# The first expert layer: the results of every other pair of experts go as rows to a scratch in DRAM and are fetched by token at the end

## The chip, the cores and the metric

The kernel runs on one core of one Trainium2 chip. The metric is the device time of one execution in microseconds (us). Shown is the median of three runs.

## The reference

Two transformer blocks are computed, each two layers deep, on 256 tokens of width 1024 with 256 tokens of context beside them, all in float32. What matters here is the mixture of experts that follows the mixer in both layers of the second block:

```
g_idx = argmax(x @ wg + bg)                  # one of 4 groups
top_p, top_e = top_k(softmax(e_logits), 2)   # two of its 8 experts
weights = g_w * top_p / sum(top_p)
hb = silu(xb @ w1[e]) * (xb @ w3[e])         # w1, w3: 1024 x 512
y = hb @ w2[e]                               # w2: 512 x 1024
out = zeros.at[tok].add(y * weights)
```

So every token goes to two of 32 experts, both of one group of eight. In the first expert layer there are 512 tokens (256 tokens and 256 of the context), in the second 256. The weights of one expert are 6 MB, those of one layer 192 MB, and each is read once.

## The kernel before

The program is a chain of blocks, one for each step of the network; a block ends when all engines have reached its end. The code touched is the function `experts`, which runs for the first expert layer (512 tokens, `by_rows` true) and for the second (256 tokens).

The router gives for each token and expert a rank (`RK`): the place that the token takes in the expert's list, or a number far too large where it doesn't go there. An expert has 64 slots (`CAP`) in a round; with these inputs one round does. Two experts make a pair (128 slots, one per partition), two pairs make a turn (`b` is 0 and 1 in it), and eight turns make the layer. The text calls the four experts of a turn e0 to e3; e0 and e1 are the pair b = 0.

For one pair:

- `pick` (VectorE) compares slot numbers with ranks into `SEL`; `indices` (TensorE) multiplies that by the tokens' numbers; `index` (VectorE) turns the product into 128 integers; `fetch` (the GpSimd queue) gathers 128 rows of 4 KB by them from the scratch `token_rows` in DRAM. `gather` (TensorE) turns those rows into `XGT`.
- For each of the two experts: `hidden` multiplies by w1 and w3 (two halves of the array side by side), ScalarE takes the silu, VectorE multiplies (`multiply`, L2399), `turn_hidden` transposes, ScalarE copies (`h_turned`), `outputs` multiplies by w2, and `y_out` copies the result, a row for each slot, to `Y2`.
- The results go back to their tokens by a product: VectorE makes the picks again, multiplied by the tokens' weights (`SELW`, L2452), TensorE transposes them (L2262), ScalarE copies them to `SWT` (L2339), and `scatter` (L2233) multiplies `Y2` by `SWT` in eight products of 128 x 512, four after the first expert's `hidden` and four after the second's. They are those of the pair before, so they lie beside the silu of the present one. `add` (L2407) adds each product, times a gate, to `X`.

After the loop one more `scatter` and `add` treat the last pair. Between them stand the squares of `X` (L2343) and their sum over all features (`sum_squares`, L2267) for the next normalisation.

The weights come in tiles of 1 MB, six per expert (`parts`): four for `hidden`, two for `outputs`. There are 16 homes for tiles; the first eight are used twice in a turn. SyncE issues all 24 loads of a turn in the order of use, each when its home's tile of before has been used:

```
for e, part in parts:
    n, lap = spot(e, part)
    sp.wait_ge(*freed(n, turns * r + i, lap))
    sp.dma_start(homes[n], weights[4 * i + e, part]).then_inc(loaded[numbers[n]].sem, 16)
```

In the trace the fetches of rows are on queue q0, the loads on q1, and the stores that ScalarE issues on q10.

Of the kernel before, what the change touches and what calls it, by code (L numbers as in the profile page):

```python
# [16 lines left out]
P = 128  # L17
# [35 lines left out]
          ("prior", EPG), ("rounds", 8), ("stream", 2), ("eps", 1), ("token", NT), ("cos_rows", 2 * ROPE), ("sin_rows", 2 * ROPE),  # L53
# [16 lines left out]
def constants():  # L70
# [52 lines left out]
    put("rounds", np.tile(np.arange(8) * CAP, (P, 1)))  # L123
    put("stream", p[:, None] % 32 == np.arange(2)[None, :])
# [35 lines left out]
def build(nc, io, out):  # L160
# [22 lines left out]
    token_rows = nc.dram_tensor("token_rows", (T, D), F32).ap()  # L183
    rows_in = [Signal(nc, f"rows_in{b}", 0) for b in range(2)]
# [20 lines left out]
    for name in ("inputs_in", "stored", "dve_step", "act_step", "squared", "summed", "rooted", "normed",  # L205
# [14 lines left out]
                 "y_copied", "weighed"):  # L220
# [1775 lines left out]
    def experts(join, layer, moe, t, by_rows):  # L1996
# [12 lines left out]
        XG = BIG[:, 0:2 * D].rearrange("p (b n) -> p b n", b=2)  # L2009
        ahead = 3 if by_rows else 2  # L2010
# [64 lines left out]
        with nc.Block() as block:  # L2075
# [5 lines left out]
            @block.gpsimd  # L2081
            def _(pool):
                join.multiplied(pool)
                nc.gpsimd.memset(Y2[:, 1, :], 0.0).then_inc(sig("cleared").sem, 1)
                nc.gpsimd.memset(SWT, 0.0).then_inc(sig("cleared").sem, 1)
                if by_rows:
                    def fetch(g, b):

                        pool.wait_ge(sig("indexed").sem, sig("indexed").at(g))
                        pool.sem_inc(sig("index_seen").sem, 1)  # L2090
                        nc.gpsimd.indirect_dma_start(XG[:, b, :], None, token_rows,
                                                     bass.IndirectOffsetOnAxis(INDEX[b][:], 0)).then_inc(rows_in[b].sem, 16)

                    pool.wait_ge(sig("rows_kept").sem, sig("rows_kept").at(16 * nt))
                    fetch(1, 1)
                    every = rounds(pool)
                    with pool.Fori(0, every) as r, pool.Fori(0, turns) as i:
                        for b in range(2):
                            fetch(2 * (turns * r + i) + b + 2, b)

            @block.sync
            def _(sp):
# [15 lines left out]
                if by_rows:  # L2118
                    sp.wait_ge(sig("rows_kept").sem, sig("rows_kept").at(16 * nt))
                    sp.wait_ge(sig("gathered").sem, sig("gathered").at(2))  # L2120
# [16 lines left out]
            def _(pe):  # L2137
# [26 lines left out]
                def gather(g, c, b, use):  # L2164

                    if by_rows and use is not None:
                        pe.wait_ge(rows_in[b].sem, rows_in[b].at(16 * (use + 1)))
                        for k in range(4 * c, 4 * c + 4):
                            last = pe_.transpose(PB[:, 4 + c, (k % 4) * P:(k % 4 + 1) * P], XG[:, b, k * P:(k + 1) * P], IDENT)
                    else:  # L2170
                        pe.wait_ge(sig("picked").sem, sig("picked").at(g + 1))
                        for k in range(4 * c, 4 * c + 4):
                            for a in range(nt):
                                last = pe_.matmul(PB[:, 4 + c, (k % 4) * P:(k % 4 + 1) * P], ATK[:, a, k * P:(k + 1) * P],  # L2174
                                                  SEL[:, a, :], start=a == 0, stop=a == nt - 1)
                    last.then_inc(sig("gathered").sem, 1)

                def indices(g):

                    pe.wait_ge(sig("picked").sem, sig("picked").at(g + 1))  # L2180
                    pe.wait_ge(sig("indexed").sem, sig("indexed").at(g - 1))
                    pe.wait_ge(sig("pick_copied").sem, sig("pick_copied").at(g - 2))
                    for a in range(nt):
                        last = pe_.matmul(PB[:, 3, T - 2:T - 1], SEL[:, a, :], con("token")[:, a:a + 1],
                                          start=a == 0, stop=a == nt - 1)
                    last.then_inc(sig("indices_made").sem, 1)
# [51 lines left out]
                gather(0, 0, 0, None)  # L2238
                gather(0, 1, 0, None)
                if by_rows:  # L2240
                    indices(1)
                every = rounds(pe)
                with pe.Fori(0, every) as r, pe.Fori(0, turns) as i:
                    turn = turns * r + i
                    for b in range(2):
                        g = 2 * turn + b
                        hidden(turn, 2 * g, g, 2 * b, b)
                        if by_rows:
                            indices(g + 2)
                        scatter(g, 1 - b, 0)  # L2250
                        turn_hidden(2 * g, 0)
                        gather(g + 1, 0, 1 - b, turn)
# [4 lines left out]
                        gather(g + 1, 1, 1 - b, turn)  # L2257
                        if by_rows:
                            pe.wait_ge(sig("indexed").sem, sig("indexed").at(g + 2))
# [19 lines left out]
            def _(act):  # L2279
# [4 lines left out]
                def keep_rows(a):  # L2284
                    act.wait_ge(sig("token_copied").sem, sig("token_copied").at(a + 1))
                    act.dma_start(token_rows[a * P:(a + 1) * P, :], ATK[:, a, :]).then_inc(sig("rows_kept").sem, 16)

                for a in range(nt):
# [3 lines left out]
                    if by_rows and a:  # L2292
                        keep_rows(a - 1)
                if by_rows:
                    keep_rows(nt - 1)
# [51 lines left out]
            def _(dve):  # L2347
# [41 lines left out]
                def index(g, b, use):  # L2389

                    dve.wait_ge(sig("indices_made").sem, sig("indices_made").at(g))
                    dve.wait_ge(rows_in[b].sem, rows_in[b].at(16 * use))
                    dve.wait_ge(sig("gathered").sem, sig("gathered").at(2 * g - 2))
                    dve_.tensor_scalar(INDEX[b][:], PB[:, 3, T - 2:T - 1], 0.25, None, ALU.add) \
                        .then_inc(sig("indexed").sem, 1)

# [36 lines left out]
                if by_rows:  # L2433
                    index(1, 1, 0)
                    pick(2)
# [3 lines left out]
                with dve.Fori(0, every) as r:  # L2439
                    with dve.Fori(0, turns) as i:  # L2440
                        for b in range(2):
# [3 lines left out]
                            if by_rows:  # L2445
                                index(g + 2, b, turns * r + i + b)
# [11 lines left out]
                            if not by_rows:  # L2458
                                dve.wait_ge(sig("gathered").sem, sig("gathered").at(2 * g + 4))
# [9 lines left out]
               group_exped=1, second_in=1, second_exped=1, dve_step=router_steps, rounds_in=1, cleared=2, logits_kept=1, logits_flipped=1,  # L2469
               rows_kept=16 * nt if by_rows else 0, squared=KD, summed=1)  # L2470
        if moe:
            return

        counted = used + loaded + [sig(n) for n in ("picked", "gathered", "indices_made", "indexed", "index_seen", "xg_copied",
                                                    "expert_silu", "expert_h", "h_flipped", "h_copied", "y_copied",
                                                    "weighed", "pick_flipped", "pick_copied", "scattered", "added",
                                                    "rank_in")]
        with nc.Block() as block:
            @block.sync
# [157 lines left out]
```

## Time and profile before

| | |
|---|---|
| median of 3 runs | 2930.11 us (2929.3 to 2930.96) |
| span of the profiled execution, first to last instruction | 2926.7 us |
| TensorE busy | 2765.9 us |
| VectorE, ScalarE, GpSimd busy | 1170.7, 707.9, 19.1 us |
| moved by DMA | 663.34 MB, mean 227 GB/s |

The page has no time of its own for the profiled execution apart from its span; the span lies 3.4 us under the median, and that is what lies around it. The page cuts the span into 40 slices of 73 us. The first expert layer is slices 23 to 30 (1603 to 2176 us), the second slices 34 to 40. In the rows, PE is TensorE, PEld its loading of weights, DVE VectorE, ACT ScalarE, POOL GpSimd and SP SyncE. A matmul in float32 stands as two instructions in the trace.

### The profile page before, as it was taken

The page shows a single profiled execution, that of the slowest core. Times are in us where ns is not written, and L with a number is a line of the kernel's source. Part 1 is how long each engine was busy: PE and PEld are TensorE (multiplying, and loading weights), DVE is VectorE, ACT ScalarE, POOL GpSimd, SP SyncE. Part 2 cuts the span into 40 slices and gives each one's busy share as a digit, 9 for nine tenths or more (in the row PEclk, how much of TensorE's full clock was granted, in tenths as well). Part 3 has the DMA queues.
Part 4 walks back from the last instruction along what each step waited for, and adds up shares of the span by engine and source line. Part 5 has one row for each costly group of instructions (what it writes and reads, how often), then busy time and mean ns, then how long its engine had stood idle before and what let it go on. Part 6 is the DMA issues. An engine that isn't in the chain of part 4 may idle for free. (4 is left out here: it accounts for less than half of the span.)

```text
span 2926.7 us, 33922 instructions
## 1 busy us (share of the span) xinstructions
PE 2765.9 (95%) x12378; PEld 1541.7 (53%) x12378; DVE 1170.7 (40%) x2630; ACT 707.9 (24%) x1347; POOL 19.1 (1%) x25
## 2 busy tenths in 40 slices
PE   5999999999999998999978999999989988999998
PEld 3555344444467777888543433333337774444444
DVE  2342477770146666771342333333343323222222
ACT  2343200000055553000251221212132222222222
POOL 0000000000000000000000000000000000000000
PEclk9999999999999999999999999999999999999999
DMA  6133455552322213775005699999923337999995
GB/s 254 74 115 115 172 216 238 234 215 82 119 73 73 67 50 136 308 291 209 0 15 225 239 401 402 406 401 402 403 113 136 138 115 284 421 422 422 421 422 235
DMA packets 101826, 663.34 MB, mean 227 GB/s; under 512 B 10608, under 2 KB 19056, under 8 KB 25072
## 3 DMA queue, kind: packets, MB, share of 16 engines
q1 hardware_dynamic: 98720, 651.22, 56.3%
q0 software_dynamic: 2448, 8.91, 0.8%
q10 hardware_dynamic: 576, 2.10, 0.2%
q8 instruction: 54, 0.88, 0.1%
q14 instruction: 28, 0.23, 0.0%
HBM read 659.04 MB, written 3.15 MB: 226 GB/s over the span
## 5 line engine op out<-in xcount | busy, mean ns | idle before, releaser
L622 PE MATMUL PB<-A,RING 128*128 128x512 f32 (+1 forms) x1408 | 459.0, 489 | 9.7 <-ACT A L499 9.7
L622 PEld LDWEIGHTS PB<-A,RING 128*128 128x128 f32 x1408 | 269.6, 192 | 199.2 <-issue 175.0
L397 DVE SCALAR_TENSOR_TENSOR WORK<-RING,MORE 128x1024 f32<-128x1024 f32 x288 | 335.4, 1220 | 20.3 <-ACT MORE L636 10.9
L451 PE MATMUL PB<-BIG,RING 128*128 (+2 forms) x928 | 310.7, 497 | 5.7 <-PEq L590 3.3
L2399 DVE TENSOR_TENSOR BIG<-BIG,PB 64x512 f32<-64x512 f32 x64 | 44.1, 690 | 671.7 <-ACT BIG L2309 671.7
L451 PEld LDWEIGHTS PB<-BIG,RING 128*128 128x128 f32 x928 | 175.9, 190 | 139.4 <-issue 128.8
L2199 PE MATMUL PB<-RING,BIG 128*64 128x512 f32 x1024 | 225.4, 592 | 0.6 <-issue 0.6
L2233 PE MATMUL PB<-BIG 128*128 128x512 f32 (+1 forms) x544 | 202.1, 504 | 11.8 <-DVE X L2407 6.9
L2407 DVE SCALAR_TENSOR_TENSOR X<-PB,MODS,X 128x256 f32<-128x256 f32 x408 | 173.3, 478 | 35.6 <-PE PB L2233 34.1
L2233 PEld LDWEIGHTS PB<-BIG 128*128 128x128 f32 x544 | 93.6, 189 | 120.6 <-issue 60.1
L514 DVE SCALAR_TENSOR_TENSOR X<-PB,MODS,X 128x256 f32<-128x256 f32 x72 | 32.4, 479 | 297.7 <-PE PB L479 296.9
L2199 PEld LDWEIGHTS PB<-RING,BIG 128*64 128x64 f32 x1024 | 75.0, 137 | 144.4 <-issue 144.3
L641 ACT ACTIVATE RS<-PB 128x512 f32<-128x512 f32 (+1 forms) x44 | 21.6, 491 | 422.1 <-PE PB L622 422.1
L2320 ACT ACTIVATE BIG<-PB 64x512 f32<-64x512 f32 x128 | 75.8, 592 | 193.7 <-PE PB L2220 192.9
L2309 ACT ACTIVATE BIG<-PB 64x512 f32<-64x512 f32 x64 | 37.7, 589 | 347.1 <-PE PB L2199 347.1
L1625 PE MATMUL PB<-A,RING 128*128 128x512 f32 x256 | 115.2, 605 | 6.2 <-ACT A L499 6.2
L2220 PE MATMUL PB<-SPARE,BIG 128*64 128x512 f32 x512 | 116.9, 598 | 1.8
L2199 PE MATMUL PB<-CST,BIG 128*64 128x512 f32 x256 | 115.3, 592 | 0.0
L2199 PE MATMUL PB<-RS,BIG 128*64 128x512 f32 x256 | 115.1, 592 | 0.0
L492 ACT ACTIVATE WORK<-X 128x512 f32<-128x512 f32 (+1 forms) x48 | 26.8, 559 | 345.2 <-DVE X L514 345.2
L1625 PEld LDWEIGHTS PB<-A,RING 128*128 128x128 f32 x256 | 48.7, 195 | 63.4 <-issue 61.8
L2174 PE MATMUL PB<-WORK,BIG 128*128 128x128 f32 x608 | 77.0, 283 | 2.3 <-DVE WORK L2385 2.3
(355 smaller groups left out, 3480.7 us busy)
## 6 DMA issues: line engine op xcount, KB each, us to landing
RING<-moe_w SPq DMA_DIRECT2D x160, 1024.0 KB, 10.7
RING<-ada_rows SPq DMA_DIRECT2D x72, 1024.0 KB, 6.8
RING<-ffn_w SPq DMA_DIRECT2D x66, 1024.0 KB, 4.8
SPARE<-moe_w SPq DMA_DIRECT2D x64, 1024.0 KB, 8.1
CST<-moe_w SPq DMA_DIRECT2D x32, 1024.0 KB, 7.7
RS<-moe_w SPq DMA_DIRECT2D x32, 1024.0 KB, 9.7
MORE<-moe_w SPq DMA_DIRECT2D x32, 1024.0 KB, 12.9
A<-moe_w SPq DMA_DIRECT2D x32, 1024.0 KB, 16.8
```

Of the source, the lines that this page charges most:

```text
L397: dve_.scalar_tensor_tensor(out=JUNK[:, n % 4, :], in0=RING[:, s, b * D:(b + 1) * D], scalar=1.0, in1=WIDE[:, side // 2, w, :], op0=ALU.mu ...
L451: last = pe_.matmul(PB[:, m, 0:tp], tile(s, 2, D)[:, r, m * P:(m + 1) * P], src(2 * i + r), start=first and r == 0, stop=False)
L622: last = pe_.matmul(PB[:, 2 * s + j, 0:t], tile(s, KD, P, j * KD * P)[:, k, :], A[:, k, 0:t], start=k == 0, stop=k == KD - 1)
L1625: last = pe_.matmul(PB[:, 1 + d, :], w[:, k, :], A[:, k, :], start=k == 0, stop=k == KD - 1)
L2174: last = pe_.matmul(PB[:, 4 + c, (k % 4) * P:(k % 4 + 1) * P], ATK[:, a, k * P:(k + 1) * P], SEL[:, a, :], start=a == 0, stop=a == nt - 1)
L2199: last = pe_.matmul(PB[m * CAP:(m + 1) * CAP, 0, :], XGT[:, b, k, slots_of(e % 2)], spot_tile(n_, 4, T)[:, k % 4, :], start=k == 0, stop=k ...
L2220: last = pe_.matmul(PB[m * CAP:(m + 1) * CAP, 2, :], HB[:, e % 2, k, :], spot_tile(n_, 2, D)[:, k % 2, m * T:(m + 1) * T], start=k == 0, s ...
L2233: pe_.matmul(result(m), Y2[:, b, m * P:(m + 1) * P], SWT[:, 0:t], start=True, stop=True) \
L2309: act_.activation(HS[CAP:P, e % 2, :], PB[0:CAP, 0, :], ACT.Silu).then_inc(sig("expert_silu").sem, 1)
L2320: last = act_.activation(Y2[slots_of(e % 2), b, m * T:(m + 1) * T], PB[m * CAP:(m + 1) * CAP, 2, :], ACT.Copy)
L2399: dve_.tensor_tensor(HS[0:CAP, j, :], HS[CAP:P, j, :], PB[CAP:P, 0, :], ALU.mult) \
L2407: last = dve_.scalar_tensor_tensor(out=X[:, m, half(w)], in0=result(m)[:, half(w)], scalar=piece(2 + moe, 5, m, w), in1=X[:, m, half(w)], ...
```

## The change

In the first expert layer only, which now has a function of its own (`experts_by_rows`; `experts` keeps the second layer):

- The pair b = 1 of each turn goes back as before, by `scatter` and `add`, now in the next turn's pair b = 0 and after the loop. `SELW`, its transposes and `SWT` are made once a turn.
- The pair b = 0 doesn't go by a product. ScalarE issues a store of its 128 rows (512 KB) from `Y2[:, 0]` to a scratch in DRAM, `result_rows` (`store_rows`).
- Before the loop VectorE computes for each token and each of its two experts the row in the scratch and the weight, zero where the expert is of a pair b = 1 (`places_back`).
- After the last fetch of the loop GpSimd's queue waits for the last store and for the last use of four homes (`MORE` and `RING` 0 and 1), and issues eight gathers of 128 rows (512 KB each) into them (`BACK`). VectorE weighs and sums the two rows of each token (`mix_rows`), and TensorE adds them to the last pair's products in PSUM, transposed by a product with the identity.
- After the loop all eight products are made in banks of their own; the sums of squares stand behind all of them.
- Two constants of 32 columns are added, and six semaphores to those cleared after the layer.

The second expert layer's code does what it did.

```diff
@@ gpsimd
+                with pool.Fori(0, every) as r:
+                    with pool.Fori(0, turns) as i:
                         for b in range(2):
                             fetch(2 * (turns * r + i) + b + 2, b)
+                    pool.wait_ge(sig("placed").sem, sig("placed").at(r + 1))
+                    for n in (10, 11, 0, 1):
+                        pool.wait_ge(used[n].sem, used[n].at(turns * r + turns))
+                    pool.wait_ge(sig("rows_stored").sem, sig("rows_stored").at(16 * (turns * r + turns)))
+                    pool.sem_inc(sig("index_seen").sem, 1)
+                    for a in range(nt):
+                        for c in range(2):
+                            nc.gpsimd.indirect_dma_start(
+                                BACK[c][:, a, :], None, result_rows,
+                                bass.IndirectOffsetOnAxis(RETURN[c * nt + a][:], 0)).then_inc(rows_back[a].sem, 16)
...
@@ tensor
+                            hidden(turn, 2 * g, g, 2 * b, b)
+                            indices(g + 2, turn)
+                            if b == 0:
+                                scatter(r, i, turn, 0)
+                            turn_hidden(2 * g, 0)
+                            gather(g + 1, 0, 1 - b, turn)
+                            outputs(turn, 2 * g, 2 * b)
+                            hidden(turn, 2 * g + 1, g, 2 * b + 1, b)
+                            if b == 0:
+                                scatter(r, i, turn, 1)
+                            turn_hidden(2 * g + 1, 1)
+                            gather(g + 1, 1, 1 - b, turn)
+                            if b == 1:
+                                pe.wait_ge(sig("indexed").sem, sig("indexed").at(g + 2))
+                                pe.wait_ge(sig("weighed").sem, sig("weighed").at(turn + 1))
+                                for a in range(nt):
+                                    last = pe_.transpose(PB[:, 3, a * P:(a + 1) * P], SELW[:, a, :], IDENT)
+                                last.then_inc(sig("pick_flipped").sem, 1)
+                            outputs(turn, 2 * g + 1, 2 * b + 1)
+
+                    done = each_round * r + KD * turns
+                    pe.wait_ge(sig("y_copied").sem, sig("y_copied").at(2 * pairs * (r + 1)))
...
+                    for m in range(KD):
...
+                        pe_.matmul(tail_result(m), Y2[:, 1, m * P:(m + 1) * P], SWT, start=True, stop=False)
+                        for a in range(nt):
+                            if m == 0:
+                                pe.wait_ge(sig("rows_mixed").sem, sig("rows_mixed").at(nt * r + a + 1))
+                            last = pe_.matmul(tail_result(m)[:, a * P:(a + 1) * P], BACK[0][:, a, m * P:(m + 1) * P], IDENT,
+                                              start=False, stop=a == nt - 1)
+                        last.then_inc(sig("scattered").sem, 1)
@@ scalar
+                def store_rows(i, g):
+                    act.wait_ge(sig("y_copied").sem, sig("y_copied").at(2 * g + 2))
+                    act.dma_start(result_rows.rearrange("(e s) n -> e s n", s=CAP)[bass.ds(2 * i, 2)],
+                                  Y2[:, 0, :]).then_inc(sig("rows_stored").sem, 16)
@@ vector
+                def places_back(c, r):
+
+                    flat = WIDE.rearrange("p a g e -> p a (g e)")
+                    every_token = [P, nt, NE]
+                    c(dve_.tensor_tensor(HOME, RK[:, :, 0:NE], con("row_base").unsqueeze(1).broadcast_to(every_token), ALU.add))
+                    for n, (one, share) in enumerate(((O1, M1), (O2, M2))):
+                        c(dve_.tensor_tensor(WIDE, wide(one, full, 2), wide(G1, full, 3), ALU.mult))
+                        c(dve_.tensor_tensor(flat, flat, con("in_rows").unsqueeze(1).broadcast_to(every_token), ALU.mult))
+                        for op, limit in ((ALU.is_ge, 0.0), (ALU.is_lt, float(CAP))):
+                            c(dve_.scalar_tensor_tensor(out=flat, in0=RK[:, :, 0:NE], scalar=limit, in1=flat, op0=op, op1=ALU.mult))
+                        c(dve_.tensor_reduce(SHARES[:, n], flat, AX.X, ALU.add))
+                        dve_.tensor_tensor(SHARES[:, n], SHARES[:, n], share[:, :, 0], ALU.mult)
+                        c(dve_.tensor_tensor(flat, flat, HOME, ALU.mult))
+                        c(dve_.tensor_reduce(PLACE[:, n], flat, AX.X, ALU.add))
+                        for a in range(nt):
+                            last = dve_.tensor_scalar(RETURN[n * nt + a][:], PLACE[:, n, a:a + 1], 0.25, None, ALU.add)
+                    last.then_inc(sig("placed").sem, 1)
+
+                def mix_rows(c, r, a):
+                    dve.wait_ge(rows_back[a].sem, rows_back[a].at(32 * (r + 1)))
+                    c(dve_.tensor_scalar(BACK[0][:, a, :], BACK[0][:, a, :], SHARES[:, 0, a:a + 1], None, ALU.mult))
+                    dve_.scalar_tensor_tensor(out=BACK[0][:, a, :], in0=BACK[1][:, a, :], scalar=SHARES[:, 1, a:a + 1],
+                                              in1=BACK[0][:, a, :], op0=ALU.mult, op1=ALU.add) \
+                        .then_inc(sig("rows_mixed").sem, 1)
```

How the order of instructions moves, at three places. In these rows `CST` is the tile with the identity, `BIG` the one that holds `XGT`, `Y2`, `SWT` and the hidden values, and `x4` counts equal instructions in a row; a matmul stands as one row here.

TensorE in the pair b = 1, from the indices to the outputs of e2, before:

```order
L2184 MATMUL PB<-CST,WORK 128x1 x4
L2232 ISA
L2233 MATMUL PB<-BIG 128x512
L2232 REGISTER_ALU
L2233 MATMUL PB<-BIG 128x512
L2232 REGISTER_ALU
L2233 MATMUL PB<-BIG 128x512
L2232 REGISTER_ALU
L2233 MATMUL PB<-BIG 128x512
L2207 MATMUL PB<-CST,BIG 128x128 x4
L2169 MATMUL PB<-CST,BIG 128x128 x4
L2218 REGISTER_ALU
```

and in the change:

```order
L2212 MATMUL PB<-CST,WORK 128x1 x4
L2235 MATMUL PB<-CST,BIG 128x128 x4
L2197 MATMUL PB<-CST,BIG 128x128 x4
L2246 REGISTER_ALU
L2248 MATMUL PB<-SPARE,BIG 64x512 x8
```

The four products of `scatter` between the indices and the transposes of the hidden values are gone; after e3's `hidden` four more are gone in the same way.

TensorE after the loop, before:

```order
L2233 MATMUL PB<-BIG 128x512
L2267 MATMUL PB<-WORK,CST 128x512 x2
L2232 REGISTER_ALU
L2233 MATMUL PB<-BIG 128x512
L2232 REGISTER_ALU
L2233 MATMUL PB<-BIG 128x512
L2232 REGISTER_ALU
L2233 MATMUL PB<-BIG 128x512
L2232 REGISTER_ALU
L2233 MATMUL PB<-BIG 128x512
L2267 MATMUL PB<-WORK,CST 128x512 x6
```

and in the change, its last two products of eight:

```order
L2301 MATMUL PB<-BIG 128x512
L2305 MATMUL PB<-CST,MORE 128x128 x4
L2300 REGISTER_ALU
L2301 MATMUL PB<-BIG 128x512
L2305 MATMUL PB<-CST,MORE 128x128 x4
L2269 REGISTER_ALU
L2269 COMPARE_AND_BRANCH
L2311 MATMUL PB<-WORK,CST 128x512 x8
```

Each product of 128 x 512 has four of 128 x 128 behind it, and all eight sums of squares stand at the end where six stood.

The GpSimd queue after the loop, in the change (before, the loop was its last work in this layer):

```order
L2104 DMA BIG<-token_rows,INDEX 128x1024
L2111 REGISTER_ALU
L2111 COMPARE_AND_BRANCH
L2114 REGISTER_ALU
L2116 ISA
L2116 REGISTER_ALU x2
L2117 ISA
L2121 DMA MORE<-result_rows,RETURN 128x1024
L2121 DMA RING<-result_rows,RETURN 128x1024
L2121 DMA MORE<-result_rows,RETURN 128x1024
L2121 DMA RING<-result_rows,RETURN 128x1024
```

Of the eight gathers four are shown; they stand behind the last fetch of the loop.

## Rows read from the trace of the kernel before

**Rows 1.** The page: DMA busy in tenths, and GB/s, in 40 slices.
```profile
DMA  6133455552322213775005699999923337999995
GB/s 254 74 115 115 172 216 238 234 215 82 119 73 73 67 50 136 308 291 209 0 15 225 239 401 402 406 401 402 403 113 136 138 115 284 421 422 422 421 422 235
```

**Rows 2.** Windows of one turn each, first expert layer: turns 3 and 8.
```profile
core 0: us, PE busy (x) PEld busy (x) DVE busy (x) ACT busy (x) POOL busy (x), PEclk, DMA share, GB/s
1769.40:1834.40 65.00, 63.69 (x282) 25.14 (x280) 21.69 (x58) 13.28 (x23) 1.87 (x2) 1.00 1.00 404
2094.40:2159.40 65.00, 63.69 (x282) 25.00 (x278) 21.94 (x59) 13.28 (x23) 1.87 (x2) 1.00 0.61 244
```

**Rows 3.** Waits of SyncE's queue, 1700 to 2130 us: total, times, longest.
```profile
SPq L2131 <- PE PB L2199: 230.5, 39, 12.7
SPq L2131 <- PE PB L2220: 103.2, 26, 6.8
```

**Rows 4.** Waits of TensorE (without its weight loads), 1770 to 2100 us.
```profile
PE PB L2233 <- DVE X L2407: 4.3, 10, 0.4
```

**Rows 5.** A window of the second expert layer's loop; columns as above.
```profile
2500.00:2800.00 300.00, 300.00 (x1570) 146.40 (x1567) 61.96 (x163) 64.83 (x116) 0.00 (x0) 1.00 1.01 421
```

**Rows 6.** DMA queues, 1770 to 2100 us: packets, MB, share of 16 engines.
```profile
q1 hardware_dynamic: 17573, 127.96, 96.1%
q0 software_dynamic: 1440, 5.24, 3.9%
```

**Rows 7.** DMA queues, 1620 to 1636 us: the four stores of `token_rows`.
```profile
q10 hardware_dynamic: 576, 2.10, 34.1%
```

**Rows 8.** Timeline of TensorE, pair b = 1: start, us, what.
```profile
1874.82 4.06 PE L2233 MATMUL PB<-BIG 128*128 128x512 f32 x8
1878.72 0.60 PE L2207 MATMUL PB<-CST,BIG 128*128 128x128 f32 x4
...
1890.32 1.99 PE L2233 MATMUL PB<-BIG 128*128 128x512 f32 x4
...
1894.56 0.60 PE L2207 MATMUL PB<-CST,BIG 128*128 128x128 f32 x4
```

**Rows 9.** Timeline of VectorE, the same stretch.
```profile
1874.67 0.69 DVE L2399 TENSOR_TENSOR BIG<-BIG,PB 64x512 f32<-64x512 f32 x1 [10.87 <-ACT BIG L2309]
1891.08 0.69 DVE L2399 TENSOR_TENSOR BIG<-BIG,PB 64x512 f32<-64x512 f32 x1 [9.51 <-ACT BIG L2309]
```

**Rows 10.** Timeline of VectorE, routing and start of the loop.
```profile
1630.22 0.29 DVE L2430 TENSOR_TENSOR WORK<-WORK 128x128 f32<-128x128 f32 x1
1647.14 0.69 DVE L2399 TENSOR_TENSOR BIG<-BIG,PB 64x512 f32<-64x512 f32 x1 [7.63 <-ACT BIG L2309]
```

**Rows 11.** Windows: the first turn's middle, and the end of the last loads.
```profile
1669.00:1677.00 8.00, 8.00 (x40) 2.67 (x38) 0.00 (x0) 1.40 (x3) 0.00 (x0) 1.00 0.09 10
2133.00:2134.00 1.00, 1.00 (x7) 0.19 (x3) 0.00 (x0) 0.00 (x0) 0.00 (x0) 1.00 0.16 66
```

**Rows 12.** Timeline of GpSimd, the last fetch.
```profile
2136.34 0.94 POOL L2091 DMA_INDIRECT BIG<-token_rows,INDEX  x1 [31.56 <-DVE INDEX L2394]
```

**Rows 13.** Timeline of TensorE, the end of the layer.
```profile
2155.96 3.65 PE L2220 MATMUL PB<-A,BIG 128*64 128x512 f32 x16
2161.08 4.07 PE L2233 MATMUL PB<-BIG 128*128 128x512 f32 x8 [1.47 <-ACT BIG L2320]
2170.52 5.31 PE L2267 MATMUL PB<-WORK,CST 128*128 128x512 f32 x12
```

**Rows 14.** Groups: line, engine, operation, shapes, count, busy us, mean ns.
```profile
L397 DVE SCALAR_TENSOR_TENSOR WORK<-RING,MORE 128x1024 f32<-128x1024 f32 x288 | 335.4, 1220 | 20.3 <-ACT MORE L636 10.9 <-DVE WORK L397 5.9 <-issue 0.9
L1499 DVE TENSOR_SCALAR WORK<-WORK,SMALL 128x512 f32<-128x512 f32 x32 | 14.1, 483 | 0.6
```

**Rows 15.** Timeline of TensorE: products of 128 x 128, second expert layer.
```profile
2609.00 1.95 PE L2174 MATMUL PB<-WORK,BIG 128*128 128x128 f32 x16
```

**Rows 16.** Windows after the layer's end: a pause of TensorE and its clock.
```profile
2180.00:2185.00 5.00, 0.00 (x0) 0.00 (x0) 4.41 (x6) 0.69 (x1) 0.00 (x0) 0.54 0.79 281
```

More of the change, by code:

```diff
@@ new lines, in experts_by_rows, with wide, across, spot @@
+        assert free[0] <= SLOT
+        router_steps, row_steps = 35, 19
+        weights = io["moe_w"][moe]
+        WTF = WT.rearrange("p a g e -> p a (g e)")
+        pairs = NE // 2
+        turns = pairs // 2
+        def wide(x, shape, axis):
+            return x.unsqueeze(axis).broadcast_to([P] + shape)
+        def across(x, n):
+            return x.broadcast_to([P, nt, n])
+        def spot(e, part):
+            n = PARTS * e + part
+            return (n, 0) if n < 12 else (n - 12, 1) if n < 20 else (n - 8, 0)
@@ new lines, in spot_tile, with freed, laps, result @@
+        def spot_tile(n, k, w):
+            return homes[n].rearrange("p (k n) -> p k n", k=k)
+        def freed(n, turn, lap):
+            return used[numbers[n]].sem, used[numbers[n]].at(turn * laps(n) + lap)
+        def laps(n):
+            return 2 if n < 4 * PARTS - SPOTS else 1
+        fit = T // t
+        def result(m):
+            return PB[:, 6 + m // fit % 2, m % fit * t:(m % fit + 1) * t]
+        each_round = KD * (turns + 1)
+        def tail_result(m):
+            return PB[:, 1 + m % 7, :]
@@ new lines, in experts_by_rows, with _, experts, take @@
+        with nc.Block() as block:
+            @block.sync
+            def _(sp):
+                for s in counted:
+                    sp.sem_clear(s.sem)
+                    sp.sem_inc(s.sem, FIRST)
+        for s in counted:
+            s.base = FIRST
+    def experts(join, layer, moe, t):
+        nt, streams = t // P, t // S
+        ATK = BIG[:, 0:NT * D].rearrange("p (a n) -> p a n", a=NT)
+        o = NT * D
+        def take(n):
+            nonlocal o
+            o += n
+            assert o <= FB * T
+            return BIG[:, o - n:o]
+        ahead = 2
@@ L2162, in _, with gather @@
                 last.then_inc(sig("ranked").sem, 1)
[L2164 to L2175, printed above, removed]
[L2176 to L2186 removed]
+                def gather(g, c):
+                    pe.wait_ge(sig("picked").sem, sig("picked").at(g + 1))
+                    for k in range(4 * c, 4 * c + 4):
+                        for a in range(nt):
+                            last = pe_.matmul(PB[:, 4 + c, (k % 4) * P:(k % 4 + 1) * P], ATK[:, a, k * P:(k + 1) * P],
+                                              SEL[:, a, :], start=a == 0, stop=a == nt - 1)
+                    last.then_inc(sig("gathered").sem, 1)
                 def hidden(turn, n, g, e, b):
```

461 lines of the change are left out of this document (394 added, 67 removed).

## The prediction

> **What bounds the kernel now.** I read the slices first, then the layer turn by turn, then who waits for whom. The slices [rows 1] show both expert layers with the DMA engines at nine tenths or more: 401 to 406 GB/s in the first, 420 to 422 in the second. So the first thing to settle is whether the first layer's loop waits for TensorE or for the weights.
>
> A window of one turn [rows 2] shows TensorE busy 63.69 of 65.0 us and the DMA share at 1.00. Both look full. The waits tell them apart: TensorE waits for no DMA at all, only for VectorE's adds, 4.3 us in 330 [rows 4], while SyncE, which issues the loads, waits for TensorE to free a home for 333.7 of 430 us [rows 3]. So today TensorE sets the turn of 65.0 us. But the transfers have almost nothing to spare. The second layer shows what 24 loads cost when nothing else is moved: 421 GB/s at a share of 1.01 [rows 5], so 1.049 MB take 2.49 us and 24 of them 59.8 us. The first layer's turn leaves 5.2 us for its two fetches of rows, 2.6 us each, and reports the engines full. The fetches' own packets explain only a part: 3.9% of 330 us for ten of them [rows 6] is 1.29 us each. The rest, 1.3 us a fetch, is either what a fetch costs the loads beside it or small gaps while TensorE holds homes back; the rows don't separate them. This is the number on which the sum hangs.
>
> **What the change takes from TensorE in the loop.** In the pair b = 1 the four products after e2's `hidden` run from 1874.82 and the transposes behind them start at 1878.72 [rows 8]. Without the products these would wait for VectorE's multiplication, which ends at 1874.67 + 0.69 = 1875.36 [rows 9]: 3.4 us less, not 3.9. After e3 the transposes move from 1894.56 [rows 8] to 1891.77 [rows 9]: 2.8 us less. The four transposes of `SELW` that go in b = 0 are at most 0.4 us. TensorE alone would need 65.0 - 6.6 = 58.4 us a turn. Eight turns save 53 us, and the loop, whose last outputs end at 2159.6 [rows 13], would end at 2107.
>
> **What the transfers allow.** They don't allow that. The engines stand still from 1669 to 1677 us (share 0.09, [rows 11]), since all homes are full until e2's `hidden` of turn 1 frees some; nothing before that point gets faster, so this gap stays. From 1677 on 7 x 24 = 168 tiles are loaded, with 14 fetches, until 2133.3 ([rows 11]: share 0.16 of the slice that begins at 2133): 168 x 2.49 = 418.3, and 38.0 over, 2.7 us a fetch. The change adds a store of 512 KB a turn, seven of which fall in this stretch (the first one falls in the gap or before). A store's own packets are 34.1% of 16 us for four [rows 7], 1.36 us each. The weights would be in at 1677 + 418.3 + 14f + 7s. With f and s at their own packets (1.29, 1.36) that is 2122.9; with 2.7 for each it is 2152.0. Even the lower one is after 2107, so in the change the loop follows the DMA engines: this is where the gain of TensorE goes. I take f = 1.9 and s = 1.6, about the middle for the fetch, because the loads' backlog will be deep and the gaps should vanish, and nearer its packets for the store, because no descriptors are made by GpSimd for it. That gives 1677 + 418.3 + 26.6 + 11.2 = 2133.1, against 2133.3 now.
>
> **The gathers at the end.** They stand behind the last fetch, which GpSimd issues at 2136.34 now, 23 us ahead of the last outputs [rows 12, 13]. In the change that is some 17 us ahead of the last weight, so fetch and gathers compete with the last loads and all share one set of engines: together they end nine transfers later, wherever they interleave. With 1.9 us each that is 2133.1 + 17.1 = 2150.2, and about 1 us to the semaphore: 2151.2. GpSimd issues one in 0.94 us [rows 12], eight in 8 us, so the queue isn't the limit.
>
> **After the loop.** For the last 128 tokens VectorE needs two passes over 1024 columns, 2 x 0.48 and 1.22 us [rows 14]: 2153.4. TensorE has then done the first product and the other three parts. The seven that are left cost each 4.07 / 4 = 1.0 us for the wide one [rows 13] and half of 1.95 us, 1.0, for its four narrow ones [rows 15]; with the last quarter of the first, 14.2 us: 2167.6. Then all eight sums of squares stand in a row, 5.31 / 6 = 0.885 us each [rows 13]: 7.1 us, 2174.7. The adds (two of 0.5 us each per product) and squares run beside. Now the same place is 2170.52 + 5.31 = 2175.8 [rows 13]. Six more semaphores to clear: +0.3. The change comes out at -0.8 us. So the tail after the last outputs grows from 16 to some 24 us and more, and the loop gives about as much.
>
> What is hidden: `places_back` is 25 short operations, the wide ones 0.29 us with a gap of 0.03 each [rows 10]; eleven of these, four sums over them (0.4 each) and ten tiny ones (0.12) come to an estimated 6.3 us. VectorE has been idle 7.63 us before the first multiplication [rows 10]. With that cover gone it would cost 6 us once. The issue of a store on ScalarE's queue has the whole of e2's `hidden` before the next silu. Behind GpSimd's new waits stands nothing until the next layer.
>
> The sum is made in the span's time; median and span lie 3.4 us apart and that is not touched. 2930.1 - 0.8 is 2929.3.
>
> **A rule against the trace.** At the end of the loop nine transfers of 512 KB are priced at 1.9 us, between 1.29 of their own packets [rows 6] and 2.7 [rows 11]. The Trainium skill (DMA: Bandwidth & Descriptors, Issuing engines are not separate DMA queues) says that DMAs started from ScalarE, SyncE and GpSimd run on the same 16 engines and interleave, and that more issuing engines save only issue time. By that rule, which speaks against moving products into transfers, the trace agrees: q0 and q1 together make the share of 1.00 [rows 6]. The same page's fit in the Trainium skill (Anatomy of one DMA) has the moving of 512 KB at bytes / 436e3, 1.2 us, the rest being latency; by that the weights would be in near 2122 and the end would be the first rival's.
>
> **The rivals.** *Transfers cost their own packets only* (f = 1.29, s = 1.36): weights at 2122.9, rows at 2122.9 + 11.6 + 1 = 2135.5, end at 2159.0, 17 us faster: 2913. For it: the packets of the fetches are no longer than others of their size [rows 6]; against it: turn after turn takes 2.6 us a fetch with the share at 1.00 [rows 2]. It decides from a mean of 1.7 on (about 30 transfers count, so 0.2 us each is the 6 us that a measurement can tell from no change, 0.2%).
>
> *Transfers cost what the turn shows* (2.7 us each, stores too): weights at 2152.0, rows at 2152.0 + 24.3 + 1 = 2177.3, end at 2200.8, 25 us slower: 2955. For it: the turns of [rows 2] with a share of 1.00, no less. It is slower by over 6 us once the mean is above 2.1.
>
> *TensorE sets the loop also in the change*, with transfers nearly free: end of the loop 2107, rows behind it at about 2115, end near 2138, 38 us faster: 2892. Only if the share of 1.00 stretches with the time there is; the second layer's 421 GB/s speaks against it.
>
> *The clock falls in the tail*: TensorE waits some 6 us for the rows between its last outputs and the last sum. After such a pause, from 2176, the granted clock was 0.54 ([rows 16]; the lower of the two levels, 1.2 GHz), so up to half of the next 7 us is lost: +3 us on the forecast, inside its range but on the slow side.
>
> **How the numbers follow.** The forecast, no change (2924 to 2936): 0.38. Transfers cheap: 0.26; TensorE-bound: 0.04. Transfers dear: 0.24; a tail that is longer for the clock or a late store: 0.08. So faster 0.30, same 0.38, slower 0.32. The range that leaves out no more than 2 in 10 reaches well into both: 2917 to 2948.
>
> **What would show it.** In the profile after: the DMA share at 1.00 through the loop with over 403 GB/s; waits of TensorE for DMA, which are not there now; turns of 64 to 66 us instead of 58.4; the last weight in near 2133 to 2140 and the rows after it; TensorE idle some 6 us after the last outputs; the last sum of squares near 2175. If turns come down to 62 us, the fetch was dear only because TensorE held the homes. If they rise over 66, a store costs the loads more than its bytes. I would be wrong altogether if the gathers, which read the same row of the scratch for every token without a stored result, were much slower than the fetches.

## The result, and the profile after

| | before | changed |
|---|---|---|
| median | 2929.7 us (2929.07 to 2930.96, 4 runs) | 2914.2 us (2911.7 to 2915.91, 4 runs) |
| span of the profiled execution | 2926.7 us | 2912.4 us |
| TensorE busy | 2765.9 us | 2727.0 us |
| moved by DMA | 663.34 MB | 671.77 MB |

The ratio is 0.9943, with a 95% interval of 0.9931 to 0.9955: 13 to 20 us faster. The forecast was no change (2929.3) with 2917 to 2948 as its range; the result lies 3 us below the range and 1 us from the time of the first rival (2913).

The page of the changed kernel, the same two lines as in [rows 1]:

```profile
DMA  6122455562222212885104799999944337999995
GB/s 256 74 113 104 169 235 216 233 242 72 95 93 73 73 59 102 306 306 190 47 15 167 268 397 421 421 421 421 421 184 144 130 124 289 421 421 422 422 421 234
```

The first expert layer (401 to 406 GB/s before) now moves 421 GB/s, as the second one always did. The share of busy time in tenths is a 9 in both. A window of ten fetches, of before:

```profile
1770.00:2090.00 320.00, 313.45 (x1377) 123.44 (x1374) 107.16 (x287) 64.58 (x112) 9.37 (x10) 1.00 1.00 403
```

and the same window of the changed kernel, with two turns of it from first fetch to first fetch (columns as in [rows 2]: PE, PEld, DVE, ACT, POOL busy, clock, DMA share, GB/s):

```profile
1770.00:2090.00 320.00, 299.40 (x1344) 118.83 (x1345) 68.68 (x176) 66.03 (x114) 9.69 (x11) 1.00 1.01 421
1769.38:1828.21 58.83, 56.05 (x262) 22.07 (x260) 13.24 (x35) 12.77 (x22) 1.87 (x2) 1.00 1.01 421
2048.77:2112.19 63.42, 58.50 (x262) 23.50 (x260) 13.25 (x36) 12.77 (x23) 1.87 (x2) 1.00 1.01 421
```

An early turn takes 58.8 us, a late one 63.4, and each figure has a cause of its own. In the early turns TensorE sets the pace, while the loads that it finds in the sixteen homes are used up faster than they come in. When that lead is gone, the transfers set it: 24 tiles, two fetches and a store are 26.74 MB, and at 421 GB/s these are 63.5 us. From then on TensorE waits for weights, which it did nowhere before [rows 4]. The waits of the changed kernel, 1770 to 2090 us (engine, line, waited for: us in total, times, longest):

```profile
PEld PB L2227 <- DMA WORK<-moe_w: 8.5, 4, 2.6
...
PEld PB L2227 <- DMA RING<-moe_w: 6.3, 8, 1.3
...
PE PB L2227 <- DMA WORK<-moe_w: 4.8, 3, 1.7
PEld PB L2227 <- DMA BIG<-moe_w: 2.4, 3, 0.9
```

The tail of the layer on TensorE, against [rows 13]:

```profile
2130.10 3.65 PE L2248 MATMUL PB<-A,BIG 128*64 128x512 f32 x16
2135.22 1.12 PE L2301 MATMUL PB<-BIG 128*128 128x512 f32 x2 [1.47 <-ACT BIG L2355]
2136.18 0.61 PE L2305 MATMUL PB<-CST,MORE 128*128 128x128 f32 x4
2137.21 0.49 PE L2305 MATMUL PB<-CST,MORE 128*128 128x128 f32 x2 [0.42 <-DVE MORE L2476]
2139.68 0.49 PE L2305 MATMUL PB<-CST,MORE 128*128 128x128 f32 x2 [1.99 <-DVE MORE L2476]
...
2152.27 7.03 PE L2311 MATMUL PB<-WORK,CST 128*128 128x512 f32 x16
```

Two stretches make the layer: from the loop's first fetch to the start of the last outputs (the loop), and from there to the issue of the next layer's first load (the tail). What lies ahead of the first fetch (1639.6 to 1645.8 us in the profiled executions) varies for all kernels, so single traces are compared by these two, worked out from the timelines:

| | loop | tail | layer |
|---|---|---|---|
| before | 516.3 | 24.0 | 540.3 |
| changed | 487.5 | 33.7 | 521.2 |

The loop gives 28.8 us and the tail takes 9.7 back: 19.1 us, just inside the measured interval.

### The profile page after: what moved, and what is told of

It reads as the page before. It is cut to its first block and busy times, and to the rows that moved or that the text cites. A ratio compares the mean times of both kernels' runs of the same rounds, so it can differ in the third digit from the quotient of the medians.

```text
span 2912.4 us, 33453 instructions
## 1 busy us (share of the span) xinstructions
PE 2727.0 (94%) x12282; PEld 1534.1 (53%) x12282; DVE 1116.7 (38%) x2471; ACT 703.5 (24%) x1339; POOL 27.1 (1%) x34
## 2 busy tenths in 40 slices
DMA packets 104131, 671.77 MB, mean 231 GB/s; under 512 B 10864, under 2 KB 19312, under 8 KB 27376
## 5 line engine op out<-in xcount | busy, mean ns | idle before, releaser
L520 DVE SCALAR_TENSOR_TENSOR X<-PB,MODS,X 128x256 f32<-128x256 f32 x72 | 32.5, 480 | 297.7 <-PE PB L485 296.9
L1631 PEld LDWEIGHTS PB<-A,RING 128*128 128x128 f32 x256 | 48.8, 195 | 63.4 <-issue 61.8
L1153 PE MATMUL PB<-RING,A 128*128 128x512 f32 (+1 forms) x192 | 71.9, 536 | 6.2 <-ACT A L505 6.2
L2714 PE MATMUL PB<-WORK,BIG 128*128 128x128 f32 x544 | 68.2, 281 | 1.0 <-DVE WORK L2901 1.0
L2763 PE MATMUL PB<-BIG 128*128 128x256 f32 x272 | 67.7, 392 | 1.5 <-ACT BIG L2836 1.5
L2450 DVE SCALAR_TENSOR_TENSOR X<-PB,MODS,X 128x256 f32<-128x256 f32 x144 | 61.9, 479 | 16.9 <-PE PB L2260 9.9
L2260 PE MATMUL PB<-BIG 128*128 128x512 f32 x128 | 63.3, 617 | 4.4 <-DVE X L2450 3.5
L2763 PEld LDWEIGHTS PB<-BIG 128*128 128x128 f32 x272 | 49.0, 190 | 33.6 <-issue 28.3
```

Source lines behind the costliest of these rows:

```text
L520: last = dve_.scalar_tensor_tensor(out=X[:, m, half(c)], in0=PB[:, m, half(c)], scalar=piece(gate_layer, gate, m, c), in1=X[:, m, half(c)] ...
L1153: last = pe_.matmul(dst.rearrange("p (a n) -> p a n", a=len(slots)), A[:, k, x], RING[:, slots[0]:slots[-1] + 1, k * S:(k + 1) * S], start ...
L1631: last = pe_.matmul(PB[:, 1 + d, :], w[:, k, :], A[:, k, :], start=k == 0, stop=k == KD - 1)
L2260: pe_.matmul(result(m), Y2[:, 1, m * P:(m + 1) * P], SWT, start=True, stop=True) \
L2450: last = dve_.scalar_tensor_tensor(out=X[:, m, half(w)], in0=of(m)[:, half(w)], scalar=piece(2 + moe, 5, m, w), in1=X[:, m, half(w)], op0= ...
L2763: pe_.matmul(result(m), Y2[:, b, m * P:(m + 1) * P], SWT[:, 0:t], start=True, stop=True) \
```

## The experiments

Three theories. Own packets: a transfer behind a deep queue of loads costs the stream its own bytes, 1.28 us for 512 KB, and the turn of before had some 2.6 us to spare although the share stood at 1.00. Dear transfers: each costs 2.6 us or so, and the engines were full at 65.0 us a turn. TensorE: it sets the loop in the changed kernel too. All times are medians, with the ratio to the kernel before (2930.45 us with the first four, 2931.02 with the next two, 2929.29 with the last three).

**One more store a turn, in the kernel before.** The 512 KB store of `Y2[:, 0]` alone, to a scratch that nobody reads.

```diff
+                def store_rows(i, g):
+                    act.wait_ge(sig("y_copied").sem, sig("y_copied").at(2 * g + 2))
+                    for x in range(1):
+                        act.dma_start(extra_rows[...], Y2[:, 0, :]).then_inc(sig("rows_stored").sem, 16)
...
+                        if by_rows and b == 0:
+                            store_rows(i, g)
```

> The kernel before with one store of 512 KB more in each of the eight turns of the first expert layer (ScalarE stores the rows of the pair b = 0 to a scratch that nobody reads). Theory Q (a transfer costs the engines its own packets, about 1.3 us, when loads are queued behind it, and the turn of 65.0 us has 65.0 - 59.8 - 2 x 1.3 = 2.6 us to spare): no change, within 2 us. Theory D (a fetch costs 2.6 us and the engines are full in the turn of 65.0 us): 8 x 1.3 to 8 x 2.6, so 10 to 21 us slower, less what the loads are ahead.

Measured: 2930.35 us, 1.0000 (0.9990 to 1.0009); loop 516.2, tail 24.1. Nothing at all. So a whole store fits into a turn that reported its engines full.

**Three stores a turn, in the kernel before.** The same with `range(3)`: 12.6 MB more in the layer.

> The kernel before with three such stores in each turn, 24 in all. Theory Q: the engines need 59.8 + 2.6 + 3 x 1.3 = 66.3 us a turn, 1.3 more than TensorE; 8 x 1.3 = 10 us, and the loads are some 17 us ahead of their use, so TensorE hardly waits: 0 to 4 us slower. Theory D: 24 x 1.3 to 24 x 2.6 less 17, so 14 to 45 us slower.

Measured: 2930.36 us, 0.9999 (0.9990 to 1.0009); loop 516.3. The same window as above, first with one store, then with three:

```profile
1770.00:2090.00 320.00, 313.85 (x1380) 123.11 (x1376) 104.93 (x282) 64.83 (x112) 9.37 (x10) 1.00 1.01 412
```

```profile
1770.00:2090.00 320.00, 313.43 (x1376) 122.99 (x1373) 106.09 (x284) 64.93 (x112) 9.36 (x10) 1.00 1.01 422
```

A share of 1.00 or 1.01 stands beside 403, 412 and 422 GB/s, at the same pace of TensorE. The three stores bring a turn to 27.8 MB, which at 422 GB/s are 65.8 us: 0.8 us more than TensorE takes, and the lead of the homes covers that for eight turns. The lead did shrink: the transfers of this loop end 502.5 us behind the first fetch, those of the kernel before 493.5 (its last fetch, which comes later still, left out), and the last outputs start at 516.3 in both. Dear transfers are refuted: at 2.6 us each, three would have made every turn some 8 us longer.

**A second store a turn, in the changed kernel.**

```diff
+                    act.dma_start(extra_rows[...], Y2[:, 0, :]).then_inc(sig("rows_stored").sem, 16)
```

> The changed kernel with a second store of the same rows in each turn, to a scratch that nobody reads. Theory Q: the loop follows the DMA engines, so each of the seven or eight stores costs its packets, 1.3 us: 9 to 10 us slower than the changed kernel (about 2924). Theory D: 2.6 us each, 18 to 21 us slower (about 2934). Theory P (TensorE sets the loop in the changed kernel): no change (2914).

Measured: 2920.37 us, 0.9962 (0.9948 to 0.9977); loop 498.0, 10.5 us longer than in the changed kernel; layer 530.1, 8.8 longer. The first fetches of two late turns, from the timeline of GpSimd:

```profile
1990.19 0.94 POOL L2105 DMA_INDIRECT BIG<-token_rows,INDEX  x1 [31.34 <-DVE INDEX L2442]
...
2054.81 0.94 POOL L2105 DMA_INDIRECT BIG<-token_rows,INDEX  x1 [31.34 <-DVE INDEX L2442]
```

The turn is 64.6 us, 1.2 more than 63.4: the store's own bytes. The whole loop gives no finer price, since 1.4 of its 10.5 us are a lower clock. TensorE waited 2.70 us for the last tile of e3's `hidden`, and from 2132 to 2136 us the granted clock was 0.50 and then 0.64; behind the same wait in the changed kernel it stayed at 1.00. The part of `hidden` that waits for this tile starts 9.1 us later behind the first fetch than in the changed kernel (490.1 against 481.0), which for seven or eight stores is 1.3 or 1.1 each.

The store that cost nothing before costs its bytes here, so the loop is bound by transfers now and was not before. That also refutes the third theory. The median lies 6.2 us above the changed kernel's 2914.2, less than the 9 to 10 expected; the changed kernel was not measured again beside this run, and the traces have 8.8.

**Every fetch twice, in the changed kernel.** The second copy goes to a tile that nobody reads.

```diff
+                    for x in range(2):
+                        nc.gpsimd.indirect_dma_start((XG[:, b, :], XTRA)[x], None, token_rows,
```

> The changed kernel with each fetch of rows issued a second time, into a buffer that nobody reads: 17 more, of which some 14 fall where the engines are full. Theory Q: 14 x 1.3 = 18 us slower than the changed kernel (about 2932). Theory D: 14 x 2.6 = 36 us slower (about 2950). Theory P: no change.

Measured: 2933.32 us, 1.0009 (0.9999 to 1.0019); loop 507.3, 19.9 us longer, layer 20.8 longer. A late turn takes 66.0 us (2066.50 to 2132.48 on the GpSimd timeline), 2.6 more than 63.4, for two fetches more: 1.3 each. Its 27.79 MB in that time are 421 GB/s again. Fetches by index, of 4 KB rows, cost the stream no more than a plain store does. Of the 19.9 us of the loop 1.7 are again a lower clock (0.50 from 2146 to 2148 us) behind the wait for the last tile.

**No gathers at the end.** Leaves out the return of half of the experts' results; all else stays, the mixing and the products too.

```diff
-                        for c in range(2):
-                            nc.gpsimd.indirect_dma_start(
-                                BACK[c][:, a, :], None, result_rows,
-                                bass.IndirectOffsetOnAxis(RETURN[c * nt + a][:], 0)).then_inc(rows_back[a].sem, 16)
+                        pool.sem_inc(rows_back[a].sem, 32)
```

> The changed kernel without the eight gathers at the end: the weighing and the sum run on what lies in the buffers, so the results of every other pair are left out of the output. It prices the gathers. Theory Q: the last four tiles come 1.3 us earlier each (5 us) and TensorE doesn't wait 2.4 us for the rows: 7 to 8 us faster than the changed kernel (about 2907). If the gathers are hidden by the last outputs: no change. If gathers cost 2.6 us each: over 12 us faster.

Measured: 2909.74 us, 0.9925 (0.9908 to 0.9942); loop 486.4, tail 32.4, layer 518.8: only 2.4 us shorter, where 7 to 8 were expected. The transfers end 483.0 us behind the first fetch instead of 493.5, so the eight gathers cost the engines 1.3 us each, no more than a fetch. But they are almost hidden. In the changed kernel q0, the queue of fetches and gathers, had 34% of the engines' time from 2116 to 2128 us and q1 67%; without the gathers it is 11% and 90%. The gathers that went ahead of the last weights made TensorE wait for e3's last tile 1.1 us longer (481.0 us behind the first fetch against 479.9), not 5. The other 1.3 us is in the tail, where TensorE still waits 1.0 us for VectorE's mixing.

**Eight idle products a turn put back, in the changed kernel.** Where the pair b = 1 had its four and four, the same products run again without a result that is used.

```diff
+                def idle_products(r, i, c):
...
+                    for m in range(4 * c, 4 * c + 4):
+                        pe_.matmul(result(m), Y2[:, 1, m * P:(m + 1) * P], SWT, start=True, stop=True)
```

> The changed kernel with eight products of 128 x 512 put back into each pair b = 1, as many as before; their results are never added. Stores, gathers and VectorE's work are those of the changed kernel. If the gain comes from TensorE's time in the loop (theories Q and D): the turn is 65 us again and the tail stays longer by 7 us: 2935 to 2938, slower than before. If it comes from anything else, the order of the loads or fewer adds on VectorE: it stays near 2914.

Measured: 2926.87 us, 0.9988 (0.9979 to 0.9998). Higher was expected (2935 to 2938). The loop is 505.5 us, 18.0 longer than in the changed kernel, with no wait of TensorE for weights. From its timeline, one half turn:

```profile
1862.47 7.04 PE L2227 MATMUL PB<-RING,BIG 128*64 128x512 f32 x32
1869.44 1.05 PE L2212 MATMUL PB<-CST,WORK 128*128 128x1 f32 x8
1870.36 3.68 PE L2268 MATMUL PB<-BIG 128*128 128x512 f32 x8
...
1885.47 3.70 PE L2268 MATMUL PB<-BIG 128*128 128x512 f32 x8
...
1893.90 2.32 PE L2227 MATMUL PB<-RING,BIG 128*64 128x512 f32 x10
```

This half, b = 1, takes 31.43 us, where the changed kernel has 26.58 (1742.80 to 1769.38 on its GpSimd timeline) and the kernel before 32.5; the other half, b = 0, takes 32.25 (32.25, 32.5). So a turn is 63.7 us and TensorE is the bound again, if only just, since its bytes need 63.4. The products' time on TensorE, less the wait for VectorE that their absence lays open, is thus 4.85 us a turn; eight turns of that are 39 us, and only 18.0 of them show, because the changed kernel runs into its transfers. The other 1.3 us a turn between this kernel and the one before, 10.8 in the loop, can be read from the two timelines. In b = 1 the stretches from the products to the transposes behind them are 3.51 and 3.54 us here and 3.90 and 4.24 before [rows 8]: the idle products wait for no adds, and that is 1.1 us. In b = 0 the four transposes of `SELW` are missing, and that half is 0.25 us shorter.

**The wide products first in the tail.** The seven products of banks 1 to 7 are made while the rows are awaited.

```diff
+                        if m == 0:
+                            for m in range(KD - 1):
+                                pe_.matmul(tail_result(m), Y2[:, 1, m * P:(m + 1) * P], SWT, start=True, stop=False)
```

> The changed kernel with the seven wide products of banks 1 to 7 made before the narrow ones that wait for the rows, while TensorE stands idle. In the profile of the changed kernel TensorE waits 2.4 us in all for the first two mixed parts. Theory (the end of the layer follows TensorE's own work behind the last outputs, with the rows' return all but hidden): that wait goes, the layer is 2 to 2.4 us shorter, about 2912 us. Rival (the rows are late and set the end): no change in the layer, since the wait only moves to the first narrow product.

Measured: 2909.87 us, 0.9933 (0.9916 to 0.9949); loop 487.4 as in the changed kernel, tail 30.8, 2.9 us shorter. TensorE's timeline has no wait for VectorE left in the tail:

```profile
2132.47 6.27 PE L2299 MATMUL PB<-BIG 128*128 128x512 f32 x14 [1.47 <-ACT BIG L2357]
2138.58 6.41 PE L2307 MATMUL PB<-CST,MORE 128*128 128x128 f32 x56
2144.83 1.02 PE L2303 MATMUL PB<-BIG 128*128 128x512 f32 x2
2145.69 1.05 PE L2307 MATMUL PB<-CST,MORE 128*128 128x128 f32 x8
2146.58 7.03 PE L2313 MATMUL PB<-WORK,CST 128*128 128x512 f32 x16
```

So with this order the rows' return is not what ends the tail; TensorE's own work does. The medians alone, 4 us apart and not taken side by side, with ratios whose intervals overlap, would not have told it.

**No empty products in the first turn.** The first turn of the loop has no pair before it, and multiplies and adds zeros. Its eight products and their adds are left out.

```diff
-                            if b == 0:
+                            if b == 0 and not (isinstance(i, int) and i == 0):
...
+                    one_turn(r, 0)
+                    with pe.Fori(1, turns) as i:
+                        one_turn(r, i)
```

> The changed kernel without the eight products and adds of the first turn, which bring back a pair that isn't there (zeros). Theory (from the second round of loads on, the loop's end follows the stream of transfers, whose start is e2's hidden part of turn 1): those products lie ahead of or inside that point, so the homes come free some 6 us earlier, the gap in the transfers shrinks from 8 to 2 us, and everything behind it comes 6 us earlier: about 2908 us. Rival (the gap is there for another reason, or the stream catches up in later turns whatever its start): the layer's length is the same, 2914 us.

Measured: 2906.97 us, 0.9920 (0.9904 to 0.9937); loop 482.9, 4.6 us shorter, layer 515.5. The first 50 us behind the first fetch, in the changed kernel and then without the empty products:

```profile
1642.62:1692.62 50.00, 48.68 (x224) 20.81 (x222) 16.96 (x56) 8.25 (x15) 2.95 (x3) 1.00 0.82 315
```

```profile
1644.10:1694.10 50.00, 45.91 (x233) 19.77 (x231) 11.57 (x43) 10.33 (x19) 2.96 (x3) 1.00 0.92 367
```

At 367 instead of 315 GB/s 2.6 MB more have come in by then, and at 421 GB/s these are 6.2 us: the gap shrinks by the 6 us that were expected. All of it is still there at the other end of the loop. The part of `hidden` that waits for e3's last tile, in the changed kernel (1642.62 is its first fetch) and without the empty products (1644.10):

```profile
2123.59 0.64 PE L2227 MATMUL PB<-WORK,BIG 128*64 128x512 f32 x1 [2.70 <-DMA WORK<-moe_w]
```

```profile
2118.79 0.64 PE L2226 MATMUL PB<-WORK,BIG 128*64 128x512 f32 x1 [2.71 <-DMA WORK<-moe_w]
```

481.0 and 474.7 us behind the first fetch: 6.3 us earlier. The last outputs start only 4.6 us earlier, because TensorE's clock fell right behind this wait, as with the second store:

```profile
2120.00:2122.00 2.00, 2.00 (x6) 0.48 (x4) 0.00 (x0) 0.00 (x0) 0.00 (x0) 0.50 0.99 408
```

From that start of `hidden` to the last outputs it is 8.2 us here and 6.5 in the changed kernel. The end of the stream is its start plus its bytes.

**Both of these.** No further edit.

> Both edits together, as the version to beat: 2906 us if they add up (8 us under the changed kernel); 2908 to 2912 if only one of them holds.

Measured: 2905.87 us (2904.91 to 2907.96), 0.9919 (0.9903 to 0.9936): 23 us below the kernel before, and the lowest median of all. Loop 482.9, tail 31.2, layer 514.1 against 521.2 in the changed kernel, 7.1 us shorter. Alone the two edits give 3.0 and 5.7 in the layer, so most of it adds up; without the empty products TensorE waits only 1.2 us for the mixed rows, and so the other edit has less to save. The clock fell here too (0.63 and 0.52 from 2116 to 2120 us), 1.7 us again. The medians don't tell this kernel from the one above.

## Why the prediction was wrong

**The step that failed** is the price of a transfer, "f = 1.9 and s = 1.6, about the middle for the fetch". Both cost their own packets: 1.3 us by the late turns of the doubled fetch, 1.2 by those of the second store, 1.3 by the missing gathers. With 14f + 7s at 1.28 the sum is 26.9 instead of 37.8, 11 us less, and nine more transfers at 1.28 instead of 1.9 take off another 5.6. That is 16.5 of the 18.3 us by which the layer came out below the forecast; most of the rest is the narrow products (below). Of the 2.6 us a fetch of before one half was bytes and the other slack.

Made again with 1.28, the sum gives the time at which the changed kernel's transfers end: 1677 + 2.9 (so much later was the first fetch in that execution) + 418.3 + 30 x 1.28 = 2136.6. In the trace:

```profile
2134.00:2136.00 2.00, 0.78 (x2) 0.49 (x3) 1.48 (x3) 0.98 (x2) 0.00 (x0) 1.00 0.91 361
2136.00:2137.00 1.00, 0.79 (x5) 0.41 (x3) 1.00 (x1) 0.00 (x0) 0.00 (x0) 1.00 0.13 53
```

They end at about 2136.1. The form of the sum held; its price did not. The price and the mechanism are those of the first rival. That its time was met within 1 us is in part luck: it takes 16.5 us off the layer, the trace has 19.1 and the medians 15.5.

**Why that slack was not seen.** The prediction took a share of 1.00 for "full". It had the number that says otherwise: 404 GB/s in [rows 2] beside 421 in [rows 5], both at a share of 1.00 or 1.01. With the bytes of a turn, 26.2 MB at 421 GB/s are 62.3 us, so 2.7 of 65.0 were free. Experiment two shows it directly, three stores for nothing.

**Point by point.**
- TensorE alone at 58.4 us a turn: 58.8 measured. Right.
- The loop follows the transfers, and TensorE waits for weights: right, but only from the end of the fourth turn on (on the GpSimd timeline 1828.21 to 1889.65 is the first turn over 58.8). Late turns take 63.4 us instead of 64 to 66, 421 GB/s.
- The gap of the first turn "stays": right, and it is what the loop's end hangs on, as the experiment without empty products shows.
- Nine transfers behind the last weight: too dear, and less of them on the path. The sum put the rows at 2151.2; the last of them were there when VectorE took them up at 2137.56 (its timeline, after a wait of 0.40 us for `RING<-result_rows`). TensorE waited 0.42 and 1.99 us for the mixed rows, where some 6 us were predicted, and taking the gathers away gave 2.4 us. The fetch and the first gathers shared the engines with the last weights, and the last outputs ended at 2133.75, so little was left to wait for.
- "GpSimd issues one in 0.94 us, eight in 8 us": one every 1.24 us, so eight in 9.6 (2113.43 to 2123.06). It cost nothing, since the transfers take as long.
- The tail: from the end of the last outputs to the last sum 16.2 us before, "some 24 us and more" predicted, 2133.75 to 2159.30 = 25.6 measured. Near in size. A product with its four narrow ones takes 1.75 us, not 2.0, since weight loads and matmuls overlap; the sums of squares 7.03 (7.1).
- `places_back` hidden: right. VectorE's first multiplication starts at 1650.03, 7.4 us behind the first fetch, as before (1647.14 against 1639.70). The issue of stores on ScalarE's queue costs nothing, as experiment one shows.
- The clock in the tail: it stayed at 1.00 in the changed kernel, with TensorE waiting 1.5, 0.4 and 2.0 us there, so that rival did not come about. With every fetch twice it did: 0.62 and 0.52 from 2162 to 2166 us, behind a wait of 1.98. And in four of the traces the clock fell where the prediction did not look for it, in the last `hidden` part of the loop.

That the Trainium skill's fit (DMA: Bandwidth & Descriptors, Anatomy of one DMA) pointed to it is borne out: 1.2 us by the page, 1.2 to 1.3 by the runs (with 1.2 the prediction's sum has the weights in at 2120.5, not "near 2122"). The other section named with it, Issuing engines are not separate DMA queues, holds as well: the second store makes the bound loop longer by its bytes, whichever engine starts it.

**What stays open.** The layer became 19.1 us shorter in the traces, the medians 15.5 us; the interval (13 to 20 us) covers both. The two profiled spans lie 14.3 us apart, since in the changed kernel's execution the first fetch came 2.9 us later and the stretch behind the layer took 1.8 us more (748.6 against 746.7). Both vary as much among the other traces, whichever kernel they are of: 1639.6 to 1645.8 us, and 746.6 to 748.7. So nothing shows that the change costs time outside the layer. Why the clock fell behind the last wait for weights in some executions and not in others is open as well.

## What to carry to other kernels

Whether DMA is full is read from GB/s beside the best that the same kernel reaches with the same size of transfers, not from the share of busy time: bytes of one turn, divided by that rate, against the turn. Where products are traded for transfers, price each transfer by its bytes while loads are queued behind it, and look for the turn in which the lead of the buffers is used up, since from there on the end is the stream's start plus its bytes; then the first thing to repair is whatever delays that start.

## What the runs showed of the hardware

The reported share of the DMA engines was 1.00 or 1.01 at 403, 412 and 422 GB/s alike. The same bytes took 4% more busy time at 403 than at 422, so packets took longer there; the share shows that something was under way, not how much more would fit. A fetch by index of 128 rows of 4 KB, started by GpSimd, a store started by ScalarE and a plain load all cost the same per byte in a full stream, 421 to 422 GB/s.

TensorE's wait of 2.7 us for the last weight tile of e3's `hidden` was followed by a granted clock near 0.5 (the lower of the two levels, 1.2 GHz) for some 3 us in four profiled executions (a second store, every fetch twice, no empty products, both edits), and by 1.00 in two (the changed kernel, the wide products first). It made that part 1.4 to 1.7 us longer, beside effects of 4.6 to 19.9 us in the loop. So a loop's length from one trace is read with the clock beside it.
